# Another order for the begin of a hybrid decoder layer: first products by terms, parameters loaded from another queue

## What is computed

```
def rms_norm(x, w):
    xf = x.astype(jnp.float32)
    y = xf * lax.rsqrt(jnp.mean(xf * xf, axis=-1, keepdims=True) + EPS)
    return (y * w.astype(jnp.float32)).astype(x.dtype)
...
    h = rms_norm(x, mix_norm_pre[i])
    proj = h @ w_in                # in hybrid_mixer
...
    qkv = jax.nn.silu(causal_dwconv(gqkv, gdn_conv))
```

## Time and profile before

| | |
|---|---|
| median of 3 runs | 1444.03 us (1443.67 to 1444.22) |
| profiled execution, own time | 1446.36 us |
| its span | 1444.6 us |
| TensorE busy | 1416.1 us (98%) |
| VectorE, ScalarE, GpSimd busy | 1031.0, 708.4, 232.8 us |
| granted clock, mean | 0.995 |

### The profile page before, as it was taken

How to read it: one execution, slowest core, us unless ns; L and a number is a source line. 1 busy time by engine, 2 the same in 40 slices (tenths; PEclk the granted TensorE clock), 3 DMA queues, 4 the chain that set the end, 5 groups by cost and what they waited for, 6 DMA issues and landing times.

```text
span 1444.6 us, 19720 instructions
## 1 busy us (share of the span) xinstructions
PE 1416.1 (98%) x7219; PEld 1188.7 (82%) x7219; DVE 1031.0 (71%) x1513; ACT 708.4 (49%) x1302; POOL 232.8 (16%) x243
## 2 busy tenths in 40 slices
PE   8999999999999999999999999999999999999996
PEld 7877788878889999888888888888888888888885
DVE  6576535643129988367997999999999685677466
ACT  6433456422248887257664443444445444454434
POOL 3000001001019777010000000000000245311010
PEclk9999999999999999999999999999999999999999
DMA  8433414544714333444442334334327765424222
GB/s 267 73 55 47 44 52 124 157 121 100 156 41 136 110 118 103 175 146 151 142 145 78 112 115 157 107 108 155 117 88 262 240 190 197 124 74 146 80 97 101
DMA packets 153104, 181.00 MB, mean 125 GB/s; under 512 B 21225, under 2 KB 92079, under 8 KB 153008
## 3 DMA queue, kind: packets, MB, share of 16 engines
q1 hardware_dynamic: 152754, 179.64, 42.2%
q10 hardware_dynamic: 254, 0.10, 0.0%
HBM read 130.43 MB, written 49.28 MB: 124 GB/s over the span
## 4 chain that ended last, share of the span: by engine, by line
PE 93%; DVE 3%; ACT 2%; issue 1%; DMA 1%; SPq 0%; POOL 0%; ACTq 0%; DVEq 0%; POOLq 0%
PE psum L2378 10%; PE psum L2380 10%; PE psum L2379 10%; PE psum L2317 4%; PE psum L2318 4%; PE psum L2319 4%; PE psum L2290 4%; PE psum L2292 4%; PE psum L2291 4%; PE psum L628 4%; PE psum L629 4%; PE psum L1302 4%; PE psum L630 4%; PE psum L683 3%; PE psum L684 3%; PE psum L685 3%
## 5 line engine op out<-in xcount | busy, mean ns | idle before, releaser
L161 DVE TENSOR_TENSOR w_wlo<-w_raw,w_whi 128x1024 fp32r<-128x1024 f32 x68 | 91.0, 1339 | 247.1 <-ACT w_whi L149 246.9
L2378 PE MATMUL psum<-m_hi,w_whi 128*128 128x512 f32 x416 | 162.4, 390 | 1.5 <-issue 0.7
L2380 PE MATMUL psum<-m_hi,w_wlo 128*128 128x512 f32 x416 | 161.9, 389 | 0.0
L2379 PE MATMUL psum<-m_lo,w_whi 128*128 128x512 f32 x416 | 161.9, 389 | 0.0
L149 ACT ACTIVATE w_whi<-w_raw 128x1024 fp32r<-128x1024 f32 x68 | 71.8, 1056 | 174.8 <-PE psum L2292 85.4
L2317 PE MATMUL psum<-w_whi,g_slot 128*128 128x512 f32 x308 | 120.1, 390 | 0.6 <-DVE w_wlo L3094 0.6
L2318 PE MATMUL psum<-w_wlo,g_slot 128*128 128x512 f32 x308 | 119.8, 389 | 0.0
L2319 PE MATMUL psum<-w_whi,g_slot 128*128 128x512 f32 x308 | 119.8, 389 | 0.0
L3092 DVE TENSOR_TENSOR g_slot<-w_raw,g_slot 128x512 fp32r<-128x512 f32 x77 | 70.8, 920 | 56.1 <-ACT g_slot L2677 56.1
L628 PE MATMUL psum<-h_hi,w_whi 128*128 128x512 f32 x256 | 102.0, 398 | 2.5 <-DVE w_wlo L161 2.5
L629 PE MATMUL psum<-h_lo,w_whi 128*128 128x512 f32 x256 | 101.1, 395 | 0.0
(11 more groups left out here) (394 smaller groups left out, 3557.8 us busy)
## 6 DMA issues: line engine op xcount, KB each, us to landing
w_raw<-in_w_up SPq DMA_DIRECT2D x39, 512.0 KB, 3.9
w_raw<-in_w_in SPq DMA_DIRECT2D x36, 512.0 KB, 6.6
s_rows<-pair_work SPq DMA_DIRECT2D x11, 1024.0 KB, 4.1
w_raw<-s_rows SPq DMA_DIRECT2D x44, 256.0 KB, 2.6
g_rows<-pair_work SPq DMA_DIRECT2D x18, 512.0 KB, 2.6
w_raw<-g_rows SPq DMA_DIRECT2D x33, 256.0 KB, 3.4
w_raw<-in_w_out SPq DMA_DIRECT2D x16, 512.0 KB, 4.3
mixed_home<-in_w_down SPq DMA_DIRECT2D x32, 256.0 KB, 3.7
```

The costliest lines, as they stand in the source:

```text
L2378: pe.matmul(out, wh[:, part], hi(kt), start=(start and kt == 0), stop=False)
L2379: pe.matmul(out, wh[:, part], lo(kt), start=False, stop=False)
L2380: ins = pe.matmul(out, wl[:, part], hi(kt), start=False, stop=(stop and kt == KT // 2 - 1))
```

## The change

Four things are changed. (a) `load_params` is called by SP, behind the load of slab 3, and no longer by ScalarE at its start. (b) `dve_row` waits for each half of the row by itself. (c) `pe_quad(0, 0, 2)` is replaced by `pe_first(term)`, eight products each: term 0 is `hi*wh`, term 1 `lo*wh`, term 2 `hi*wl`. Term 0 needs no low part and no remainder. Groups 0 of tiles 0 and 1 are turned ahead of it, groups 1 only after it; ScalarE and VectorE follow in that order. (d) The turned tiles use banks 4 to 7 alone, so that the four banks of products need no tile to leave first.

```diff
@@ sp
         for j in range(3, first["f"]):
             self.slabs.load(sp, j)
+            if j == 3:
+                self.load_params(sp)
             for dst in zero_to[2 * (j - 3):2 * (j - 2)]:
@@ pe
-        self.pe_turn(pe, 0)
-        self.pe_turn(pe, 1)
-        self.pe_quad(pe, 0, 0, 2, range(2))
+        self.pe_turn(pe, 0, (0,))
+        self.pe_turn(pe, 1, (0,))
+        self.pe_first(pe, 0)
+        self.pe_turn(pe, 0, (1,))
+        self.pe_turn(pe, 1, (1,))
+        self.pe_first(pe, 1)
         self.pe_turn(pe, 2)
-        self.pe_quad(pe, 0, 0, 2, range(2, NH))
+        self.pe_first(pe, 2)
         self.pe_turn(pe, 3)
@@ pe_turn
-            b = 2 * t + g if t < 4 else 4 + (2 * t + g) % 4
+            b = 4 + (2 * t + g) % 4
@@ dve_row
-        self.multiplied.wait(dve, ("row", 1))
         for n in range(2):
             key = ("row", n)
+            self.multiplied.wait(dve, key)
@@ new
+    def pe_first(self, pe, term):
+
+        if term == 0:
+            pe.wait_ge(self.slabs.rounded, 1)
+            pe.wait_ge(self.s["rounded_x"], 2)
+        elif term == 1:
+            for t in range(2):
+                self.banks.released(pe, ("x", t, 0))
+        else:
+            self.slabs.ready(pe, 0)
+        part = slice(0, 2 * P)
+        for m in range(NH):
+            key = ("g", m, 0)
+            out = (self.banks.open(pe, key, m) if term == 0 else self.banks.of(key))[:, part]
+            for kt in range(2):
+                wh, wl = self.slabs.halves(0, kt * DG + m * P, P)
+                pe.matmul(out, wl if term == 2 else wh, (self.lo if term == 1 else self.hi)[:, kt, part],
+                          start=(term == 0 and kt == 0), stop=False)
@@ act
-        self.load_params(act)
         act.wait_ge(s["made"], 4)
         k.table(act, ACT.Sqrt)
         self.act_norm(act, 0)
         self.act_norm(act, 1)
+        self.act_x(act, 0, (0,))
         slabs.round(act, 0, m_)
-        self.act_x(act, 0)
-        self.act_x(act, 1)
+        self.act_x(act, 1, (0,))
+        self.act_x(act, 0, (1,))
+        self.act_x(act, 1, (1,))
         self.act_norm(act, 2)
@@ dve
+        self.dve_lo(dve, 0, (0,))
         slabs.remainder(dve, 0)
-        self.dve_lo(dve, 0)
-        self.dve_lo(dve, 1)
+        self.dve_lo(dve, 1, (0,))
+        self.dve_lo(dve, 0, (1,))
+        self.dve_lo(dve, 1, (1,))
         self.dve_x(dve, 2)
```

More of the change, by code:

```diff
@@ L350, in sp, with load_params @@
             self.slabs.load(sp, first["q"] + NH + 1 + j)
-    def load_params(self, act):
+    def load_params(self, sp):
         a, s = self.a, self.s
@@ L358, in load_params @@
                         (C_GCONV, a["gdn_conv"].rearrange("o k (r c) -> (o k r) c", c=P))):
-            act.dma_start(self.rows[at:at + src.shape[0], :], src).then_inc(s["loaded"], 16)
+            sp.dma_start(self.rows[at:at + src.shape[0], :], src).then_inc(s["loaded"], 16)
         fsrc = a["ffn_conv"].rearrange("o k (r c) -> (o k r) c", c=P)
@@ L362, in load_params @@
         for i in range(2):
-            act.dma_start(self.frows[0:half, i, :], fsrc[i * half:(i + 1) * half, :]).then_inc(s["loaded"], 16)
+            sp.dma_start(self.frows[0:half, i, :], fsrc[i * half:(i + 1) * half, :]).then_inc(s["loaded"], 16)
     def sp_chunk(self, sp, c):
@@ L553, in pe_chunk_turn, with pe_turn @@
         self.multiplied.mark(ins, ("a_turn", c))
-    def pe_turn(self, pe, t):
+    def pe_turn(self, pe, t, groups=range(2)):
         pe.wait_ge(self.s["scaled"], t + 1)
-        for g in range(2):
+        for g in groups:
             key = ("x", t, g)
-            b = 2 * t + g if t < 4 else 4 + (2 * t + g) % 4
+            b = 4 + (2 * t + g) % 4
             out = self.banks.open(pe, key, b)
@@ L702, in act_norm, with act_x @@
                        scale=1.0 / DM).then_inc(self.s["rooted"], 1)
-    def act_x(self, act, t):
-        for g in range(2):
+    def act_x(self, act, t, groups=range(2)):
+        for g in groups:
             key = ("x", t, g)
@@ L915, in dve_x, with dve_lo @@
                                  op1=ALU.mult).then_inc(s["scaled"], 1)
-    def dve_lo(self, dve, t):
-        for g in range(2):
+    def dve_lo(self, dve, t, groups=range(2)):
+        for g in groups:
             key = ("x", t, g)
-            dve.wait_ge(self.s["rounded_x"], 2 * t + g + 1)
+            dve.wait_ge(self.s["rounded_x"], 2 * t + g + 1 if t > 1 else 2 * g + t + 1)
             here = lambda ap: ap[:, 4 * g:4 * g + 4, t * P:(t + 1) * P]
```

## The result

| | before | changed |
|---|---|---|
| median of 20 runs each | 1446.11 us (1443.66 to 1448.31) | 1448.01 us (1445.28 to 1451.00) |
| ratio, 95% interval | | 1.0017 (1.0010 to 1.0023) |
| profiled execution, own time | 1446.36 us | 1447.14 us |
| its span | 1444.6 us | 1445.4 us |
| TensorE busy | 1416.1 us | 1415.3 us |

The change makes the kernel slower by 1.4 to 3.3 us, 2.5 us in the middle; the medians stand 1.9 us apart. The interval leaves no change out, yet the size is under the 0.2% (2.9 us) named in the prediction. The first three runs of before, the only ones shown until then, lie at 1443.67 to 1444.22 and so 2.1 us under the median of twenty.

What follows compares the result with a forecast made beforehand. The prediction took the kernel as TensorE-bound, busy 98% of the span. TensorE turning tile 3 2.2 us late, added to the shown runs' median of 1444.03, gave 1446.2 us, range 1443.0 to 1447.9.

Steps and rivals of the forecast that it cites:

- step (6): Tile 2's transposes and third term end at 20.9; TensorE waits 0.8 us, turning tile 3 at 21.75 instead of 19.56.
- three signs that the prediction had named for being wrong: Square of tile 2 before 14.5, no second TensorE wait for `x_tiles`, or clock column dropping between 19 and 25 us.
- steps (3) and (4): Second groups' transposes follow the first products, ending at 15.4; ScalarE's square of tile 2 behind them comes 2.8 us later.
- rival B: Later half-clock stretches, after waits at 89 to 92 and 172 to 174, are dodged: 1.5 us back each; chance 0.14.
- rival C: TensorE's clock rises early, with products from 11.8: 1444.5 us; chance 0.12, counted together with the change doing nothing.
- The bound of 1.7 us: Clock rising before the second groups' transposes saves 1.7 us on eight products and eight transposes, leaving +0.5 us.
- Rival A: New TensorE waits before tiles 2 and 3 also drop its clock, adding 1.2 to 1.5 us: 1447.4 to 1447.7; chance 0.2.

Runs made afterwards that it cites:

- terms alone: Changed kernel with parameters loaded by ScalarE at its start and the row copied after both halves again; ratio 1.0022 to the kernel before.
- both kernels with a move: Changed kernel with squares of tiles 2 and 3 ahead of the second groups, ratio 0.9995; or with second groups turned ahead of the first term's products, 0.9990.
- small parts alone: Kernel before with only parameters loaded by SP behind slab 3 and the row copied by halves; ratio 1.0002, median 1445.72 us.

## Why the prediction was right and wrong

**The mechanism was right up to tile 2, and step (6) came out by luck.** The first transpose was forecast for 8.4 and came at 8.37; the first product for 11.8, came at 11.66; the square of tile 2 for 16.0, came at 15.67; the wait before tile 2 at 2.3 us ended at 19.2, was 2.6 us ended at 18.71. Tile 3 was forecast 2.2 us late and was 2.4 us late; the ratio says 2.5 us. But two of the three signs that the prediction had named for being wrong came true in this profile: no second wait for `x_tiles`, and a clock column at half until 21.5 us (it fell at 18.1; the sign was set for 19 to 25). Step (6) had a wait of 0.8 us before tile 3; in its place stand slow products. Tile 3 was scaled at 21.19, 0.4 us ahead of the forecast, and without the fall could have been turned at about 21.3 (an estimate from this row and the 0.06 us before tile 2); the fall put it at 21.92, near the 21.75 forecast. That everything hangs on the second groups standing behind the first products, and the square behind them, steps (3) and (4), held in both experiments that undo one of the two.

**The number was wrong: 1446.2 with a range to 1447.9, measured 1448.01.** The step that failed is the base of the sum, where the difference of 2.2 us was put on a median of 1444.03. That is the level of three runs; of twenty, the median is 1446.11, and 2.2 on top of it is 1448.3. The shown profiled execution, 1446.36, stood by the twenty and not by the three, and its clock rows named a reason: two stretches of 1.5 us each. I used them for rival B and argued from three runs within 0.55 us that nothing flips from run to run. Twenty runs show two groups, seven at 1443.7 to 1444.3 and twelve at 1445.8 to 1446.7, and the account above shows executions of one and of two falls. No execution of before in the lower group was profiled, but the mean granted clock of each execution is on record: of the 66 beside the experiments, the 22 under 1444.6 us have 0.996 to 0.998, and of the 44 over 1445.4 us 40 have 0.995 or less. One fall (1.6 us in 1445) is 0.001. So the two groups differ in the clock; that the difference is one certain fall, near 90 or at 174, stays argued.

**The early rise of the clock (rival C) came, in small.** It rose at about 14.7 in the changed kernel and not at 17.6; this took some 0.3 us off the second groups, and is why the square came 0.3 us ahead of the forecast. The bound of 1.7 us needed a rise before 13.5.

**Rival A happened, at 0.7 us in one profile and at 1.1 us in another.** In the changed kernel the clock fell at about 18.1, in the new wait, for 0.7 us, since the rest ran into the second wait. In "terms alone", with the same order, it fell at 21.2. Tile 3 was scaled at 22.27 and turned at 22.33, so nothing was lost up to there; behind it, to the fifth slab's products, it is 47.1 us, against 46.0 in the changed kernel and in the kernel before. That fall cost 1.1 us. So the price hangs on where the fall lies. The times vary from run to run too: of the changed kernel's 20 executions six took 1449.4 to 1451.0 us, with clocks of 0.992 to 0.995, and two 1445.3 and 1445.4, with 0.998; of "terms alone", four of 11 took 1450.1 to 1450.6 with 0.994. Only one of those slow ones was profiled, the one of 1450.22 us with three falls; that the others have three as well is argued. The prediction kept A out of the forecast and gave it 0.2. Filling the wait held the clock up in the one execution profiled. The rule of the Trainium skill ("TensorE: Matmul & The Clock Gate", "Part 1: The HAM clock gate") that an idle array goes back to half clock agrees with this trace; but the trace also shows a wait of 2.5 us without a fall, the one near 90 us of the changed kernel.

**Rival B happened in the profiled execution** (one fall instead of two) and hid 1.6 of 2.4 us. Who reads only the two spans, 1444.6 and 1445.4, sees a third of the loss.

**Parameters, row copy and banks.** Costed at nothing, 0.6 us and nothing. No run takes the banks by themselves; both kernels with a move keep them and lose nothing. The parameters were first read at 45.9, issued by 21.2, and slab 4 was issued at 22.06. The small parts alone moved slab 0's rounding from 9.83 to 9.28, which I had held fixed; why the slab was there sooner is not shown. Together they were worth 0.3 us at tile 3, within the noise of the ratio.

## What to carry to other kernels

When an engine's list is written by hand, an early start of one engine's work is bought with the delay of whatever it now stands in front of; follow that to the next engine whose own list has something unrelated queued behind the delayed result (here a square that needed none of it), since there the price is paid. Here the same products by terms lost 2.5 us with that square behind the delayed result and gained 2.0 us with it ahead and the transposes no longer delayed. And where times of a kernel fall in groups, take the base of a forecast from the profiled execution and the count of its slow stretches, not from the first few runs.

## What the runs showed of the hardware

- A fall to half clock costs TensorE at full load 1.6 us (lateness of the same products, 2.37 to 0.73 us, where one trace has the fall and the other not), and an account of ten executions closes with it; it followed the wait of 2.5 us near 90 us in seven of the eight profiled executions that had that wait, and not in the changed kernel's (91.4 to 94.8: 0.92 us of work in 3.4, no fall).
- Eleven unread 512-column products in that wait took 2.69 us, and the clock stayed up there in both profiled executions that had them.
- Seven small DMA issues that took 0.23 to 0.58 us each on ScalarE's queue took up to 1.97 us for one behind the large loads on SP, with no effect on the time.
